# Compression matmuls put in turn with a part of the output projection

## What is computed

```
xn = rmsnorm(h, norm_g[i]); proj = xn @ w_in[i]          # split into hq, hf, hi, ..., kcm, vcm, ...
y_hg = (gated recurrence over 64-row chunks, 4 heads)    # 512 columns: "the recurrence's rows"
def compress(kv, pe, w1, w2):                            # 31 overlapping blocks of 32 rows
    flat = (kv[:, :, idx, :] + pe).reshape(B, G, NC, 32 * 64)
    return silu(flat @ w1) @ w2                          # w1: 2048 x 128
kc, vc = rmsnorm(compress(kcm, ...)), compress(vcm, ...) # 2 groups
y_nsa = (attention over kc, vc, selected blocks and a window, gated)   # 512 columns
h = h + concat([y_hg, y_nsa]) @ w_out[i]                 # 1024 x 1024
h = h + sigmoid(rmsnorm(h) @ w_pg[i]) * (p[i] @ w_pp[i])
```

## Time and profile before

| | us |
|---|---|
| median of 3 runs | 2848.05 |
| lowest, highest | 2847.53, 2849.46 |
| the profiled execution | 2847.53 |
| its span | 2845.7 |
| mean granted clock of TensorE | 0.987 |

### The profile page before, as it was taken

How to read it: one execution, slowest core, us unless ns; L and a number is a source line. 1 busy time by engine, 2 the same in 40 slices (tenths; PEclk the granted TensorE clock), 3 DMA queues, 4 the chain that set the end, 5 groups by cost and what they waited for, 6 DMA issues and landing times.

```text
span 2845.7 us, 41439 instructions
## 1 busy us (share of the span) xinstructions
PE 2745.1 (96%) x13652; PEld 2290.9 (81%) x13652; DVE 1170.9 (41%) x2130; ACT 1273.4 (45%) x2187; POOL 1388.2 (49%) x1713
## 2 busy tenths in 40 slices
PE   8999899999989999999999999999999999999998
PEld 6889668888966878887887888888888788888887
DVE  4767752476775234332232421313442324242232
ACT  5554644555564452544443532324354544343233
POOL 4525445442544444455453554555445464365453
PEclk9999899999989999999999999999999999999999
DMA  5223002322300232233332333333223333232332
GB/s 151 71 53 93 17 22 91 87 74 55 92 14 29 91 100 81 82 88 101 117 104 75 97 97 97 96 98 109 74 82 104 97 119 97 60 112 96 97 96 97
DMA packets 269796, 242.47 MB, mean 85 GB/s; under 512 B 29376, under 2 KB 201600, under 8 KB 269568
## 3 DMA queue, kind: packets, MB, share of 16 engines
q1 hardware_dynamic: 266672, 235.12, 28.1%
q10 hardware_dynamic: 2896, 4.52, 0.5%
HBM read 237.51 MB, written 2.10 MB: 84 GB/s over the span
## 4 chain that ended last, share of the span: by engine, by line
PE 66%; issue 17%; POOL 13%; ACT 2%; DVE 1%; DMA 0%; POOLq 0%; DVEq 0%; ACTq 0%
PE bank L1934 11%; PE bank L1938 11%; PE bank L1937 11%; POOL wlo L2773 11%; PE bank L1868 8%; PE bank L1872 8%; PE bank L1871 8%; PE bank L1823 1%; PE bank L814 1%; PE bank L817 1%; PE bank L818 1%; PE bank L2059 1%; PE bank L2025 1%; POOL Ql L2762 0%; POOL vv L2762 0%
## 5 line engine op out<-in xcount | busy, mean ns | idle before, releaser
L2773 POOL TENSOR_TENSOR wlo<-raw,whi 128x256 fp32r<-128x256 f32 (+1 forms) x1616 | 1293.0, 833 | 1318.8 <-ACT whi L2083 1318.5
L2083 ACT CAST whi<-raw 128x1024 fp32r<-128x1024 f32 (+2 forms) x443 | 455.7, 1034 | 619.1 <-PE bank L1934 405.4
L1868 PE MATMUL bank<-xhi,whi 128*128 128x512 f32 x928 | 364.4, 393 | 1.9 <-DVE h L2465 1.6
L1872 PE MATMUL bank<-xhi,wlo 128*128 128x512 f32 x928 | 361.9, 390 | 0.0
L1871 PE MATMUL bank<-xlo,whi 128*128 128x512 f32 x928 | 361.6, 390 | 0.0
L1934 PE MATMUL bank<-whi,xhi 128*128 128x512 f32 x832 | 326.7, 393 | 7.0 <-DVE xlo L2356 7.0
L1938 PE MATMUL bank<-whi,xlo 128*128 128x512 f32 x832 | 324.1, 390 | 0.0
L1937 PE MATMUL bank<-wlo,xhi 128*128 128x512 f32 x832 | 323.8, 389 | 0.0
L814 PE MATMUL bank<-whi,xhi 128*128 128x512 f32 (+2 forms) x704 | 259.7, 369 | 5.8 <-DVE pT L1451 3.1
L817 PE MATMUL bank<-wlo,xhi 128*128 128x512 f32 (+2 forms) x704 | 255.0, 362 | 0.0
L818 PE MATMUL bank<-whi,xlo 128*128 128x512 f32 (+2 forms) x704 | 254.7, 362 | 0.0
(11 more groups left out here) (502 smaller groups left out, 4885.1 us busy)
## 6 DMA issues: line engine op xcount, KB each, us to landing
raw<-in_w_in SPq DMA_DIRECT2D x147, 512.0 KB, 3.6
raw<-in_w SPq DMA_DIRECT2D x132, 512.0 KB, 3.8
raw<-in_w_pg SPq DMA_DIRECT2D x16, 512.0 KB, 3.8
raw<-in_w_o SPq DMA_DIRECT2D x16, 512.0 KB, 3.8
raw<-in_xa_k SPq DMA_DIRECT2D x16, 512.0 KB, 3.8
raw<-in_xa_v SPq DMA_DIRECT2D x16, 512.0 KB, 3.8
raw<-in_xa_q SPq DMA_DIRECT2D x16, 512.0 KB, 3.9
raw<-in_xa_o SPq DMA_DIRECT2D x16, 512.0 KB, 3.8
```

The lines of the kernel that those rows point to most:

```text
L1868: mm = pe.matmul(o, wh, rhs[0][:, k, :], start=(k == 0), stop=False)
L1872: mm = pe.matmul(o, wl, rhs[0][:, k, :], start=False, stop=(k == KD - 1))
L2083: nc.scalar.copy(whi[:, j % SLOTS, 0:nk * cols], raw[:, j % SLOTS, 0:nk * cols]).then_inc(hi_split, 1)
L2773: ins = nc.gpsimd.tensor_tensor(wlo[:, s, part], raw[:, s, part], whi[:, s, part].bitcast(F32), ALU.subtract)
```

## The change

The first four k-tiles of the output projection (the part for the recurrence's rows) for columns 0 to 511 leave `out0`, which keeps the k-tiles 4 to 7. They come as two blocks (`beside` 0 and 1) of four k-tiles by 256 columns. In `step_c_hid` TensorE now does in each of the 8 rounds three matmuls of 256 columns (stationary data from `xhi` and `xlo`, moving data from the `beside` block) and the three of 62, in turn. Four new PSUM results (`be`, banks 1 to 3) are added to `h` by VectorE in four `out_add` steps. `out1` and `out0` change places behind the attention, and with them the banks of some results. The cast of weight blocks in this stretch is no more tied to the step but has its own places in the list (`round`).

```diff
+BESIDE = [("w_out", 0, HG, 256 * c, 256) for c in range(2)]
...
-    s += hid[0][:1] + [("nz_gate", 0), ("q_rot",)] + hid[0][1:] + [("k_turn",)] + hid[1][:1] + [("q_rope",)] + hid[1][1:]
-    s += [("nz_exp", 1), ("c_out",), ("nz_gate", 1)]
+    hid, beside = hid[0] + hid[1], [("beside", c, BESIDE[c]) for c in range(2)]
+    s += hid[:1] + [("round", hid[0]), ("nz_gate", 0), ("q_rot",)] + beside[:1] + hid[1:2] + [("round", beside[0]), ("k_turn",)]
+    s += hid[2:3] + [("round", hid[1]), ("round", hid[2]), ("out_add", 0), ("q_rope",)] + beside[1:] + hid[3:] + [("round", beside[1])]
+    s += [("nz_exp", 1), ("round", hid[3]), ("c_out",), ("out_add", 1), ("out_add", 2), ("nz_gate", 1), ("out_add", 3)]
...
-    out0 = tm("out0", "w_out", 0, 512)
+    out0 = tm("out0", "w_out", 0, 512, tiles=HG, k0=HG)
...
-    s += main + [("p_turn",)] + out0[:1] + last[0] + last[1] + out0[1:]
-    s += out1[:2] + [("turn_low", "ple")] + out1[2:] + pp[0] + [("turn_high", "ple"), ("sums", "ple")]
+    s += main + [("p_turn",)] + out1[:1] + last[0] + last[1] + out1[1:2] + out0
+    s += out1[2:3] + [("turn_low", "ple")] + out1[3:] + pp[0] + [("turn_high", "ple"), ("sums", "ple")]
...
@@ turn_groups
+    low, high = (LOW, HIGH) if step[1] == "ple" else (HIGH, LOW)
...
@@ groups_one
-        high = 4 * (step[1] in ("out0", "pp0", "pg0"))
+        high = 4 * (step[1] in ("out1", "pp1"))
...
-        return [(("ch", step[1]), (0,))] if step[2] == 0 else []
+        return ([(("ch", step[1]), (0,))] if step[2] == 0 else []) + [(("be", 2 * step[1] + step[2]), (1, 2, 3))]
...
@@ TensorE, step_c_hid
+                e = chunk(("beside", w, BESIDE[w]))
                 if i == 0:
                     pe.wait_ge(*clo_ready.next(l))
                     pe.wait_ge(*G.free(name, l))
+                if (w, i) == (0, 0):
+                    pe.wait_ge(*G.evacuated(("yT", HG - 1), l))
+                pe.wait_ge(*G.free(other, l))
...
+                    half, k = divmod(j, HG)
+                    tt = 2 * i + half
+                    x, y_ = xhi[:, k, tt * P:(tt + 1) * P], xlo[:, k, tt * P:(tt + 1) * P]
+                    eh, el = whi[:, e, k * 256:(k + 1) * 256], wlo[:, e, k * 256:(k + 1) * 256]
+                    q_ = G.ps(other)[:, 256 * half:256 * (half + 1)]
+                    mm = pe.matmul(q_, x, eh, start=(k == 0), stop=False)
                     if j == 0:
+                        mm.then_inc(chunk_begun, 2 if (w, i) == (1, 0) else 1)
+                    pe.matmul(o, wh, a, start=(i == 0 and j == 0), stop=False)
+                    pe.matmul(q_, x, el, start=False, stop=False)
+                    mm = pe.matmul(q_, y_, eh, start=False, stop=(k == HG - 1))
+                    if j == 7:
+                        mm.then_inc(*G.full(other))
+                    mm = pe.matmul(o, wh, b, start=False, stop=False)
+                    if j == 7 and (w, i) == (1, 1):
                         mm.then_inc(chunk_begun, 1)
...
@@ ScalarE, the walk through the steps
-                if step in number1:
+                if step[0] == "round":
+                    high_part(act, l, chunks1, ring1, number1[step[1]] + HIGH_LEAD)
+                elif step in number1 and step[0] not in ("c_hid", "beside"):
                     high_part(act, l, chunks1, ring1, number1[step] + HIGH_LEAD)
...
@@ VectorE
+            def step_out_add(step):
+                c, half = divmod(step[1], 2)
+                name = ("be", step[1])
+                at = h[:, 2 * half:2 * half + 2, 256 * c:256 * (c + 1)]
+                dve.wait_ge(*G.filled(name, l))
+                tt_(at, at, G.ps(name)[:, :].rearrange("p (t n) -> p t n", t=2), ALU.add).then_inc(*G.empty(name))
```

More of the change, by code:

```diff
@@ L383, in numbered @@
 def numbered(steps):
-    chunks = [s for s in steps if s[0] in ("fm", "tm") or s[0] == "c_hid"]
+    chunks = [s for s in steps if s[0] in ("fm", "tm") or s[0] in ("c_hid", "beside")]
     return {s: j for j, s in enumerate(chunks)}, [s[-1] for s in chunks]
@@ L1529, in step_tm @@
                     elif kind[:3] == "out":
+                        if kind == "out0" and tt == 0:
+                            for n in range(4):
+                                dve.wait_ge(*G.evacuated(("be", n), l))
                         at = h[:, tt, int(kind[3]) * T:(int(kind[3]) + 1) * T]
```

14 lines of the change are left out of this document (5 added, 9 removed).

## The result

| | before | after |
|---|---|---|
| median, us (lowest, highest) | 2848.76 (2847.53, 2851.91) | 2882.95 (2879.70, 2883.76) |
| span of the profiled execution, us | 2845.7 | 2881.2 |
| mean granted clock | 0.987 | 0.977 |
| compression stretch, layer 0 / layer 1, us (start of the first to start of the last 62-column matmul) | 22.25 / 18.97 | 44.39 / 43.13 |

The changed kernel is slower by 34 us: ratio 1.0116, 95% interval 1.0100 to 1.0132. I had forecast 2857.4 and a range up to 2867, so the direction was right and the size was not: 34 us against 9.

A forecast was written before the change was run, and what follows sets the result against it. TensorE, busy 96% of the span, was taken as the bound. Full-clock stretch, waits and removed work (-0.1 and +3.2 us by layer), clock 2 x 2.8 and tail 2 x 0.3 gave +9.3: 2857.4 us, range 2850 to 2867.

The forecast's parts named there:

- What bounds the kernel and the prices: TensorE's row sets the time; at full clock a 62-column matmul costs 0.112 us, a 256-column one 0.120, each paying its load.
- Rival A: Mixed row: loads hide under dense neighbours, a pair costs 0.141 us instead of 0.232, time 2839.9 us; chance 0.07.
- Term 2: Ahead of the first compression step: TensorE waits for VectorE's last xlo evacuation, +4.2 us in each layer.
- Term 3: Ahead of the third compression step: a weight cast now behind the first result's gate brings 3.4 us of new waiting per layer.
- The work taken away: Later output projection: 48 matmuls of 512 columns fewer per layer, 10.9 us on the path.
- term 5: Behind the stretch: later compressed keys and additions to h delay the attention, +0.3 us per layer, bounds -2 and +2.9.
- Term 4: Compression stretch: 2 to 5 us at half clock after the first wait, plus a possible second fall; +2.8 us per layer.
- rival D: Compression stretch: the mixed row doesn't raise the clock, 10.2 us per step, up to 2892 us; chance 0.10, mostly shorter kinds.
- a second fall: Wait ahead of the third step: the clock falls again in perhaps two cases of three, 1.5 us each, so 1.0.
- On the transposes: Rows of 16 transposes: the trace shows the clock rising there, against the skill page; by the page the sum is 1.0 us higher.

The follow-up runs named there:

- before_wait: Kernel before, with only the new wait of TensorE for the last xlo evacuation ahead of the first compression matmul; 2861.33 us, ratio 1.0044.
- unmixed: Changed kernel, but each compression step does its 24 matmuls of 256 columns first, then the 24 of 62; 2863.1 us, ratio 1.0044.
- wide4: Changed kernel, with each small matmul streaming its 62 columns four times over (248 columns); 2864.92 us, ratio 1.0057.
- turn_early: Changed kernel, with the recurrence's rows transposed and split one block earlier, ahead of the last block of nz; 2869.77 us, ratio 1.0075.
- wide2: Changed kernel, with the small matmuls widened to 124 columns; 2869.52 us, ratio 1.0079.
- late_adds: Changed kernel, with ScalarE's c_out work ahead of two casts and the exponentials, and three additions to h later; 2881.05 us, ratio 1.0116.
- wide4_no_waits_tail: Changed kernel with 248-column small matmuls, early beside 1 cast, rows transposed early, c_out earlier and three additions to h late; 2845.39 us, ratio 0.9988.
- cast_early: Changed kernel, with ScalarE's cast of weight block beside 1 ahead of the gate of the first compression result; 2869.97 us, ratio 1.0075.
- before_wide4: Kernel before, with only the compression matmuls streaming their 62 columns four times over (248 columns); 2848.46 us, ratio 0.9999.

## Why the prediction was right and wrong

**What bounds the kernel and the prices** held. 0.213 us per mixed matmul at half clock and 0.115 at full were the prediction's 0.213 and 0.116. Rival A (the loads hide) is out: a pair costs 0.23, not 0.141.

**Term 2, the wait at the start** (+4.2 per layer): 5.52 against 1.26 us is +4.3, and before_wait shows that the evacuations alone are enough to cause it. The prediction named only those. In the changed kernel the new block's `wlo` ends 0.07 us later still, so taking away one of the two would have gained next to nothing.

**Term 3, the wait in the middle** (3.4): the time at which TensorE could go on held. From the end of the second step (293.10) the gate began at +0.28, the cast ended at +2.0 and GpSimd's last piece at +4.9, as these rows of ScalarE and GpSimd show, and TensorE went on at +5.20:

```profile
293.38 0.22 ACT L1161 ACTIVATE et<-bank 128x62 f32<-128x62 f32 x1 [19.12 <-PE bank L1031]
...
294.08 1.03 ACT L2115 CAST whi<-raw 128x1024 fp32r<-128x1024 f32 x1
```

```profile
295.19 2.78 POOL L2805 TENSOR_TENSOR wlo<-raw,whi 128x256 fp32r<-128x256 f32 x4 [18.49 <-ACT whi L2115]
```

The bracket says 1.53 us in place of 3.4 only because the transposes beside it took twice as long at half clock; where the clock was full ahead of it (unmixed, wide4, turn_early) it is 3.2 to 3.3.

**The work taken away** (-10.9): from the first block of the output projection behind the attention to the first compression step of layer 1, before:

```profile
406.13 0.50 PE L814 MATMUL bank<-whi,xhi 128*128 128x512 f32 x1 [1.56 <-DVE pT L1451]
```

and after:

```profile
433.57 0.50 PE L820 MATMUL bank<-whi,xhi 128*128 128x512 f32 x1 [1.56 <-DVE pT L1473]
```

That is 357.95 us to 764.08, and 352.11 to 785.68, so -5.8; with +4.3 for the wait at its end, 10.1 went away (the 1.8 of term 5 is counted apart, since these rows begin behind it).

**Term 4, the clock, is the step that failed.** I wrote "I take 2 to 5 us at half clock, 4 as the middle", from a row of the recurrence in which work after an idle time had the clock back in 2.9 us. It was back after 38.7 us in layer 0, and after 24.0 for 3.4 us and then again after 37.6 in layer 1. In layer 0 three of the four steps ran at 10.2 us in place of 5.6, in layer 1 two at 10.2 and the third at 8.8. The stretch was 44.4 and 43.1 us where the sum at the full clock was 29.0: 15.4 and 14.1 us of clock per layer, against my 2.8, that is 23.9 us more than forecast over the two layers. It is rival D in nearly its full form (2892 by the prediction), to which I gave 0.10, "mostly the shorter kinds". The mistake was to take the way back from a row of other work, when the price of the return depends on what the row holds. The rows of this very stretch spoke against me: in the kernel before the small matmuls stayed at half clock for 17 us and came out of it in transposes. I used them against D ("the 62-column steps with transposes got the clock back too"), where they should have set the size. The second mistake was to count the two falls apart. In layer 0 the clock was low from the first wait on, and the wait in the middle could take nothing more; in layer 1 transposes had brought it back, and 1.56 us of idle ahead of a mixed row were followed by another fall. The chance that I gave to a second fall, two in three, was fair: in the four kernels in which the clock was full ahead of that wait (unmixed, wide4, wide2, turn_early) it fell in or right behind it in six of eight cases.

**Term 5, behind the stretch** (+0.3, bounds -2 and +2.9): the first block of the output projection stood 116.6 us behind the last small matmul, 114.8 before, +1.8, within the bounds. The transpose of the compressed keys (L1048) comes 7.26 us behind the last small matmul, 6.24 before, so +1.02 for the +1.05 of the prediction. TensorE's wait ahead of it grew by more, from 0.42 us to 3.88, since TensorE came to it earlier, now at the full clock:

```profile
324.25 0.47 PE L1048 MATMUL bank<-ident,Ql 128*128 128x128 f32 x1 [3.88 <-DVE Ql L1759]
```

In ScalarE's order two casts, which are new there, and the exponentials, which stood there before, lie between 318.0 and 321.7 us ahead of its part of `c_out`, as I had said. One reading of the prediction was wrong: TensorE did not work at half clock until 305.73 in the kernel before, the clock was back at 302.3 (0.84 over 302 to 303). late_adds took that wait away and got little for it (2 us, within the error), wide4_no_waits_tail more.

The sum by what was measured: waits 2 x 4.3, stretch +22.1 and +24.2, work taken away 2 x -10.1, tail 2 x 1.8 gives 38.3 for 35.5 measured. The 2.8 us left over are for the most part ahead of layer 0's first step, which came 0.7 us early even with its wait, and behind layer 1, where -10.3 stands for the -8.3 of the sum. I have no cause for them.

**On the transposes** the rows went on speaking against the page. In the stretches of the changed kernel the clock came back only in rows of 16 transposes (at 311.3, 809.7 and 823.3), as in layer 0 of the kernel before. The Trainium skill (TensorE: Matmul & The Clock Gate, PE-mode transpose) says that the full clock doesn't engage in transpose mode. This trace disagrees, if not each time: the transposes at 293.10 in layer 0 did not bring it back. One reserve: the kernel calls them as transposes (`pe.transpose`) and the trace prints them as MATMUL with `ident`, so it doesn't show whether they run in the mode that the page means.

## What to carry to other kernels

Price a clock change from rows of the same kind of work as the one you put there, not from the nearest return of the clock elsewhere: with the same wait ahead the return took 3 to 5 us in dense work or with the small matmuls at 248 columns in turn with it, 10 to 11 with them at 124, and over 20 at 62, and then in or right behind transposes. Small matmuls with a fresh load of stationary data each had columns nearly for free (0.112 us for 62, 0.120 for 248; that the load sets this price is my reading and was not tested by itself). So widening them by reading the operand several times kept the clock without moving any work, once nothing else held TensorE up there. And a stretch that gets faster meets waits that its slowness had hidden (3.5 us for a shared PSUM bank here), so look for those in the same edit.

## What the runs showed of the hardware that I had not expected

The same matmuls of 256 and 62 columns in turn kept the full clock for two steps (11 us in turn_early, 12 with transposes between in cast_early) when they found it so, and left it at 1.2 GHz for two steps and more when they found it low, with the engine busy all the time in these steps in both cases. Idle time ahead changes the first half of that: found at full behind 1.56 to 3.2 us of idle, the clock was gone 0.3 to 1.7 us into the step (changed kernel in layer 1, late_adds and turn_early). The Trainium skill (TensorE: Matmul & The Clock Gate, What's actually happening) says that "the default state is throttled, and activity releases the throttle". The trace agrees as far as the idle time goes; but PE and PEld busy for 1.00 over 292 to 293 us at a clock of 0.50 show that the busy time in the profile does not tell whether the clock comes back. What decides it these runs do not settle: they changed the width of the small ones and their order, and both mattered. The same wait of 3.5 us was followed by a fall in one layer of before_wide4 and not in the other. Nor do they tell why the transposes got the clock back in most places and not in all.
